# Mixture-of-experts stage: another order of the experts, two of them cut into 64 and 32 rows, and array tiles for the last two blocks and the products at the end

## The reference

```python
# hier_moe: t is (256, 1024); w_gate, w_up (32, 1024, 512); w_down (32, 512, 1024)
g_prob = softmax(t @ w_group + b_group); g_idx = argmax(g_prob)        # 4 groups
e_prob = softmax((t @ w_expert + b_expert)[group g_idx])               # 8 experts in the group
top_p, top_i = top_k(e_prob, 2)                                        # 2 experts for each token
top_w = g_gate * top_p / sum(top_p)
y = sum over the token's 2 experts e:  top_w * (silu(t @ w_gate[e]) * (t @ w_up[e])) @ w_down[e]
out = x + y
```

## Time and profile before

| | us |
|---|---|
| median of the runs | 1901.54 |
| the profiled execution itself | 1901.3 |
| its span, first to last instruction | 1899.5 |
| TensorE busy (matmul) | 1756.2 |
| VectorE busy | 1000.1 |
| ScalarE busy | 637.1 |
| first load of the experts' weights issued | at 1361.50 |
| first matmul of the first expert | at 1374.69 |
| granted TensorE clock, mean | 0.974 |

### The profile page before, as it was taken

The page is one execution under the profiler, slowest core; times in us unless marked ns, Lnnn a source line. Parts: engine busy times, 40 slices in busy tenths (PEclk is TensorE's granted clock), DMA queues, the critical chain, the costliest instruction groups (busy, mean ns, idle before and its releaser), DMA issues.

```text
span 1899.5 us, 22022 instructions
## 1 busy us (share of the span) xinstructions
PE 1756.2 (92%) x8277; PEld 1149.3 (61%) x8277; DVE 1000.1 (53%) x1751; ACT 637.1 (34%) x1140; POOL 93.3 (5%) x98
## 2 busy tenths in 40 slices
PE   7998999999999999999999998889699999966788
PEld 6887777777888877777774545554444443322232
DVE  5988555545678875555665896542522222111112
ACT  5543555454455445544534111220211111100001
POOL 1000000000000000000002121000000000000001
PEclk9999999999999999999999998989899999999899
DMA  7544434445555354443565343224388999999996
GB/s 244 167 145 132 145 112 134 115 123 162 149 178 176 111 166 122 120 137 100 169 182 162 110 155 100 83 73 129 128 334 373 368 395 420 420 420 421 420 421 246
DMA packets 131497, 392.60 MB, mean 207 GB/s; under 512 B 15567, under 2 KB 17379, under 8 KB 106817
## 3 DMA queue, kind: packets, MB, share of 16 engines
q1 hardware_dynamic: 126752, 386.64, 57.9%
q0 software_dynamic: 4640, 4.56, 0.8%
HBM read 387.73 MB, written 10.43 MB: 210 GB/s over the span
## 4 chain that ended last, share of the span: by engine, by line
PE 66%; DMA 13%; DVE 13%; ACT 4%; issue 3%; SPq 0%; POOL 0%; DVEq 0%; ACTq 0%; POOLq 0%
PE bank L749 11%; PE bank L698 10%; PE bank L700 10%; PE bank L699 10%; PE bank L1147 7%; PE bank L1164 5%; DMA r<-in_w_gate 3%; DVE w_lo L1251 3%; DMA spare<-in_w_gate 3%; DMA spare<-in_w_up 3%; DMA w_raw<-in_w_up 2%; DVE r L1251 2%; DVE r L1257 2%; PE bank L825 2%; PE bank L666 2%
## 5 line engine op out<-in xcount | busy, mean ns | idle before, releaser
L1251 DVE TENSOR_TENSOR w_lo<-w_raw,w_hi 128x1024 fp32r<-128x1024 f32 x266 | 320.7, 1217 | 225.4 <-ACT w_hi L2237 224.6
L698 PE MATMUL bank<-w_hi,h_hi 128*128 128x512 f32 x800 | 327.2, 409 | 14.4 <-DVE w_lo L1251 14.4
L2237 ACT CAST w_hi<-w_raw 128x1024 fp32r<-128x1024 f32 x266 | 277.5, 1048 | 164.3 <-PE bank L700 157.1
L700 PE MATMUL bank<-w_hi,h_lo 128*128 128x512 f32 x800 | 316.1, 395 | 0.0
L699 PE MATMUL bank<-w_lo,h_hi 128*128 128x512 f32 x800 | 315.5, 394 | 0.0
L698 PEld LDWEIGHTS bank<-w_hi,h_hi 128*128 128x128 f32 x800 | 152.6, 191 | 51.2 <-issue 15.2
L700 PEld LDWEIGHTS bank<-w_hi,h_lo 128*128 128x128 f32 x800 | 152.2, 190 | 33.7
L699 PEld LDWEIGHTS bank<-w_lo,h_hi 128*128 128x128 f32 x800 | 152.7, 191 | 29.1
L749 PE MATMUL bank<-w_raw,h_all 128*128 128x512 f32 (+1 forms) x320 | 142.4, 601 | 1.1 <-DVE h_all L1251 1.1
L2408 ACT ACTIVATE r<-bank,small 128x256 f32<-128x256 f32 (+1 forms) x152 | 63.8, 425 | 207.0 <-DVE small L1254 207.0
L2108 DVE TENSOR_REDUCE gate_t<-bank 128x128 f32<-128x512 f32 (+1 forms) x26 | 18.0, 692 | 189.4 <-PE bank L1129 189.4
(11 more groups left out here) (354 smaller groups left out, 2419.0 us busy)
## 6 DMA issues: line engine op xcount, KB each, us to landing
w_raw<-in_w_in SPq DMA_DIRECT2D x236, 512.0 KB, 3.7
w_raw<-in_w_proj SPq DMA_DIRECT2D x48, 512.0 KB, 3.7
r<-in_w_gate SPq DMA_DIRECT2D x20, 1024.0 KB, 22.2
r<-in_w_up SPq DMA_DIRECT2D x20, 1024.0 KB, 20.5
spare<-in_w_gate SPq DMA_DIRECT2D x19, 1024.0 KB, 23.2
spare<-in_w_up SPq DMA_DIRECT2D x18, 1024.0 KB, 20.8
spare<-in_w_down SPq DMA_DIRECT2D x14, 1024.0 KB, 23.8
w_raw<-in_w_down SPq DMA_DIRECT2D x14, 1024.0 KB, 25.9
```

Of the source, the lines that this page charges most:

```text
L698: e.matmul(out_, sh, mh, start=first, stop=False, skip_group_check=shared)
L700: return e.matmul(out_, sl, mh, start=False, stop=last, skip_group_check=shared)
L1251: o.did(v.tensor_tensor(out_, a, b, op), sem, value)
L2237: a.copy(halves(n)[0], raw_of(n)).then_inc(w_hi, 1)
```

## The change

- `RANKS` is another order. Before: 0, 15, 16, 1, 17, 18, 2, 19, 20, 3, 21, 4, 22, 5, 23, 6, 24, 7, 25, 8, 26, 9, 27, 10, 28, 11, 29, 12, 13, 14, 30, 31. After: four small ranks (15 to 18) behind rank 0, four (19 to 22) behind rank 1, three (23 to 25) behind rank 2, one behind each of ranks 3 to 6, and ranks 7 to 14 one after the other; 14, 30, 31 stay last.
- Ranks 5 and 6 become two blocks, of 64 and of 32 rows, in place of one of 128: 37 blocks.
- `FLAT` goes: `outer` of the last two blocks puts its two halves of the output side by side, in one bank, and ScalarE copies it in one instruction of 128 x 512.
- The products at the end take the output's first 512 columns from partitions 0 to 63 and the others from 64 to 127, so the two matmuls of a token tile stand in different rows of the array. The weights' matrix is made on all 128 partitions for that. The four adds and stores go by token tile first.
- Small tables move to make room for 37 columns in place of 35.

```diff
-RANKS = [0, 15, 16, 1, 17, 18, 2, 19, 20, 3, 21, 4, 22, 5, 23, 6, 24, 7, 25, 8, 26, 9, 27, 10, 28, 11, 29, 12, 13, 14, 30, 31]
-PARTS = {0: (0, P), 1: (0, P), 2: (0, P)}
+RANKS = [0, 15, 16, 17, 18, 1, 19, 20, 21, 22, 2, 23, 24, 25, 3, 26, 4, 27, 5, 28, 6, 29, 7, 8, 9, 10, 11, 12, 13, 14, 30, 31]
+PARTS = {0: (0, P), 1: (0, P), 2: (0, P), 5: (0, P // 2), 6: (0, P // 2)}
...
-    return P // 4 if most <= P // 4 and rank < EXP - 2 and FOUR else P // 2 if most <= P // 2 else P
+    return P // 4 if most <= P // 4 and rank < EXP - 2 else P // 2 if most <= P // 2 or PARTS.get(rank, (0,))[-1] == P // 2 else P
...
-                    n, ways = ROWS[x], 1 if FLAT[x] else WAYS[x]
+                    n, ways = ROWS[x], WAYS[x]
...
-                                done = e.transpose(bank[0:P // 2, c:c + P], last_by_token[:, w, t, :], ident)
+                                done = e.transpose(bank[:, c:c + P], last_by_token[:, w, t, :, :].rearrange("p d s -> p (d s)"), ident)
...
-                for n in range(2):
-                    await_drained(("down", last_blocks[0], n))
-                    for t in range(T):
+
+                def weighted(w, t, n, bank):
+                    part = slice(n * P // 2, (n + 1) * P // 2)
+                    return e.matmul(bank[:, :], last_weights[part, w, t, :], y_out[last_blocks[w] % 2][part, 0:CH], start=w == 0, stop=w == 1)
+
+                await_drained(("down", last_blocks[0], 0))
+                for t in range(T):
+                    for n in range(2):
                         _, bank = take(ends, ("end", t, n))
-                        e.matmul(bank[:, :], last_weights[:, 0, t, :], y_out[last_blocks[0] % 2][0:P // 2, n * CH:(n + 1) * CH], start=True, stop=False)
+                        weighted(0, t, n, bank)
                 outer(BLOCKS - 1, 0)
                 outer(BLOCKS - 1, 1)
...
+                await_drained(("down", last_blocks[1], 0))
+                for t in range(T):
+                    for n in range(2):
+                        weighted(1, t, n, banks[acc[("end", t, n)][0]]).then_inc(ends_summed, 1)
...
-                tt(of_last, of_last, last_by_token[:, 1, :, :], ADD)
-                o.prev()
-                tt(last_by_token, of_last.unsqueeze(1).to_broadcast([P, 2, T, P // 2]), last_mask.unsqueeze(2).to_broadcast([P, 2, T, P // 2]), MUL, last_in)
+                tt(of_last, of_last, of_second, ADD)
+                o.prev()
+                for i in range(2):
+                    tt(last_by_token[:, :, :, i, :], of_last.unsqueeze(1).to_broadcast([P, 2, T, P // 2]), last_mask.unsqueeze(2).to_broadcast([P, 2, T, P // 2]), MUL,
+                       last_in if i else None)
...
-                if WAYS[x] == 1 or FLAT[x]:
+                if WAYS[x] == 1:
```

More of the change, by code:

```diff
@@ L68 @@
 WAYS = [P // n for n in ROWS]
-FLAT = [r >= EXP - 2 for r in BLOCK_RANK]
 LOAD = [RANKS.index(r) for r in BLOCK_RANK]
@@ L574, in build @@
         last_blocks = (BLOCKS - 2, BLOCKS - 1)
[L575 to L578, removed]
+        last_by_token = scratch[1][:, :].rearrange("p (w t d s) -> p w t d s", w=2, t=T, d=2)
+        of_last, of_second = (scratch[3][:, i * P:(i + 1) * P].rearrange("p (t s) -> p t s", t=T) for i in range(2))
+        last_mask = scratch[3][:, 2 * P:3 * P].rearrange("p (w s) -> p w s", w=2)
+        last_weights = scratch[0][:, :].rearrange("p (w t s) -> p w t s", w=2, t=T)
         own_rows = [[R[i][:, 0:D], R[i][:, D:2 * D]] for i in (3, 6)]
@@ L589, in build @@
         block_rank, block_skip, block_last = (bias_rows[0][:, i * BLOCKS:(i + 1) * BLOCKS] for i in range(3))
-        count, offset = bias_rows[0][:, 108:140], bias_rows[0][:, 140:172]
+        count, offset = bias_rows[0][:, 116:148], bias_rows[0][:, 148:180]
         chosen_bf = nc.alloc_sbuf_tensor_at("chosen", [P, 2 * T * EXP], BF16, offset=starts["bias0"] + 4 * 240)
@@ L596, in build @@
         key = bias_rows[0][:, 432:464]
[L597 to L600, removed]
+        placed = bias_rows[1][:, 116:244].rearrange("p (c e) -> p c e", c=2)
+        position = bias_rows[1][:, 244:248]
+        start_f, before, beyond = (bias_rows[1][:, 248 + 38 * i:248 + 38 * i + BLOCKS] for i in range(3))
+        key_col, rank_col, count_col, offset_col = (bias_rows[1][0:EXP, 442 + i:443 + i] for i in range(4))
         expert_i = bias_rows[1][:, 464:464 + BLOCKS].bitcast(I32)
-        offset_all, count_all = (bias_rows[0][:, c:c + BLOCKS] for c in (304, 172))
+        offset_all, count_all = (bias_rows[0][:, c:c + BLOCKS] for c in (304, 180))
         order_cols = scratch[2][0:EXP, 0:EXP + 3 * BLOCKS]
         ahead, ahead_count = scratch[2][0:EXP, 160:192], scratch[2][0:EXP, 192:224]
-        position_i = bias_rows[1][:, 376:380].bitcast(I32)
-        start_i = bias_rows[1][:, 384:384 + BLOCKS].bitcast(I32)
-        row_i = bias_rows[1][:, 424:424 + BLOCKS].bitcast(I32)
+        position_i = bias_rows[1][:, 362:366].bitcast(I32)
+        start_i = bias_rows[1][:, 366:366 + BLOCKS].bitcast(I32)
+        row_i = bias_rows[1][:, 404:404 + BLOCKS].bitcast(I32)
         unit_row, lane, index_row = consts[:, 1088:1216], consts[:, 1267:1268], consts[:, 1218:1250]
@@ L2150, in moe @@
                         b, n, bank = await_full(("last",))
[L2151 removed]
+                        o.did(v.tensor_copy(last_weights.rearrange("p w t s -> p (w t s)"), bank[:, :]), drained[b], n)
                 for t in range(T):
@@ L2157, in moe @@
                 o.prev()
-                for n in range(2):
-                    for t in range(T):
-                        v.wait_ge(ends_summed, n * T + t + 1)
+                for t in range(T):
+                    for n in range(2):
+                        v.wait_ge(ends_summed, t * 2 + n + 1)
                         bank = banks[acc[("end", t, n)][0]]
@@ L2862, in sync_program @@
                         s.dma_start(PLACES[q % len(PLACES)], source[:, j * 2 * D:(j + 1) * 2 * D]).then_inc(in_moe[q % len(PLACES)], 16)
-            for n in range(2):
-                for t in range(T):
-                    s.wait_ge(x_final, n * T + t + 1)
+            for t in range(T):
+                for n in range(2):
+                    s.wait_ge(x_final, t * 2 + n + 1)
                     s.dma_start(out[t * P:(t + 1) * P, n * CH:(n + 1) * CH], x3[:, t, n * CH:(n + 1) * CH]).then_inc(stored, 16)
```

4 lines of the change are left out of this document (1 added, 3 removed).

## The result

| | before | after |
|---|---|---|
| median of the runs, us | 1901.12 (1899.32 to 1904.47, 4 runs) | 1886.32 (1884.05 to 1890.23, 4 runs) |
| the profiled execution, us | 1901.3 | 1886.12 |
| its span, us | 1899.5 | 1884.3 |
| mean granted clock | 0.974 | 0.972 |

The medians are 14.8 us apart, where 15.6 were forecast and 1885.9 was the predicted median. The ratio of the runs is 0.9917, with a 95% interval of 0.9897 to 0.9937, which is 15.8 us off, between 12.0 and 19.6.

What follows compares the result with a forecast made beforehand. The weight stream bounds the kernel: its start, its stops and the tail behind the last up piece set the end. Stream 6.7 plus tail 8.9 gives 15.6 us off 1901.3, 1885.7, or 1885.9 as a median; forecast's range 1882.7 to 1890.5.

Steps and rivals of the forecast that it cites:

- The bound: From 1580 us TensorE waits for the DMA; 421 GB/s, the most any window shows, is the stream's full rate.
- The first dip: Stream's stop at 1410 to 1424 us, waiting for rank 0's down piece: 9.6 us lost, unchanged by the new order.
- The second dip: Stream's stop at 1465 to 1481 us, waiting for rank 1's down piece: moves to about 1497, shrinks from 11.2 to 7.2 us.
- 2 to 3.5 us for a stretch: Length of TensorE's low clock (1.2 GHz) behind a wait, costing half its length; 1.7 us taken at rank 1.
- The third dip: Stream's stop at 1520 to 1538 us, 2.9 us lost: goes, with 3 us to spare at rank 2.
- The order's gain: Stream from the new expert order: 11.2 + 2.9 - 7.2 - 0.2 = 6.7 us earlier; bounds 2.1 to 9.3.
- The tail: Work behind the last up piece: 8.9 us shorter through faster outer and end products; bounds 6.8 to 9.5.
- The dip only moves: Rival: rank 1's new stop is as long as the two it replaces (14.1 us), only the end gains, 1892.6; chance 0.16.
- More goes: Rival: clock stays up behind rank 18, rank 1's stop under 4 us, small frictions go: 1880 to 1882; chance 0.10.
- Slower: Rival: rank 1 meets a cold TensorE whose clock stays at 1.2 GHz through both blocks, up to 1930; chance 0.03.
- The tiles that don't overlap: Rival at the kernel's end: end products' tiles don't overlap, 1888.0, or the last outer products' column tiles don't, 1892.8.

Runs made afterwards that it cites:

- The experiment with the five products: Kernel after, plus five unused 128x512 matmuls of constants in TensorE's idle time ahead of rank 1's first piece: 1883.0 us, ratio 0.9895 to the kernel before.

## Why the prediction was right, point by point

**The whole.** 14.8 us between the medians against 15.6 forecast. The profiled executions differ by 15.2, of which 1.0 is the untouched front; the two terms of the forecast's sum measure 5.2 and 9.0, 14.2 together. So the mechanism held, one term was 1.5 us too large, and that the predicted median (1885.9) is met within 0.4 us is in part luck.

**The bound.** The stream sets the time from 1377 us on, and what counts is where it stands still. The experiment with the five products holds to that: 2.5 us off a stop were 2.5 us off the stretch. The cut of ranks 5 and 6 took 6.5 us of work from TensorE and nothing from the time. One reading was too strict: 421 GB/s is not the most that any window shows (1366 to 1410 before has 422, windows of 2 us up to 430), but every stretch of 25 us and more without a stop lies at 420 to 422.

**The first dip** was to stay at 9.6 us and has 10.0 in a window of the same length. With its edges it is 9.9 before and 11.0 after, by the earlier issue told above and not by the order.

**The second dip** is the mis-sized term: 7.2 forecast, 8.7 measured. The forecast had the load issued 48.0 us behind rank 1's first matmul (46.0, 1.7 for the clock, 0.3 to the issue); it took from 1452.87 to 1502.25, 49.4. Of these 1.4 us, 0.8 are the clock: the first piece took 6.14 us for 3.60, so 2.5 in place of 1.7. The step that failed is "2 to 3.5 us for a stretch", worked out by spreading a mean of 0.95 over more than ten waits. Such a mean has short stretches in it beside long ones; the row behind a wait of about this length was a short stretch, as a window that follows the one shown there tells:

```profile
1668.00:1670.00 2.00, 2.00 (x16) 1.46 (x16) 1.00 (x2) 0.27 (x1) 0.00 (x0) 0.72 1.05 430
```

A mean of 0.72 is 1.1 us at the lower level, so there the clock came back some 3.1 us behind the first matmul. At rank 1 it stayed at 0.50 over all of 1451 to 1457, and the 2.5 us lost are 5.1 us of work at that level, an estimate from 6.14 and 3.60. This was no accident of one execution: in the six profiles with a wait of 4.75 to 5.17 us ahead of rank 1 the piece took 6.04 to 6.32. The experiment with the five products gave this loss back whole, 2.5 us. The other 0.6 are differences of about 0.1 us in each of the six terms between summed rows and the real row of two blocks.

The page "TensorE: Matmul & The Clock Gate" of the Trainium skill warned in its section "Why this matters for your kernels" against idle gaps between bursts of matmuls. The trace agrees: behind the gap of 4.89 us the clock was 0.50, and with the gap filled it was 1.00.

**The third dip** was to go and went: 420 GB/s from 1508 to 1580. Rank 2's first piece again met a low clock (5.15 us behind a wait of 4.76), and here it cost nothing, as the forecast had it with its 3 us to spare.

**The order's gain** by these steps: 6.7 forecast; measured 2.5 from the second dip (11.2 to 8.7) and 2.7 from the third (2.9 to 0.2), which is the 5.2 of the stretch, alone and in the whole change alike. The 0.2 that the forecast took off for more scatters is below what the rounded rates can show.

**The tail:** 8.9 forecast, 9.0 measured. Outer products 3.45 each, measured 3.60 and 3.65 with their drains; end products 1.9 each, measured 1.99. The gathered rows were there: the weighted adds began at 1872.97 behind the last three short operations, with no wait for them. The last four adds were counted at 0.74 each and took 0.60 from start to start, 2.48 together. The price was read wrongly: the pair of 1.48 in the earlier trace rows was not VectorE's own pace, its second add came when its product was done, and TensorE started its products 0.86 to 0.96 us apart. That made up for the small differences elsewhere.

**The rivals.** The dip only moves (14.1 us): fell, 8.7. More goes (a warm clock behind rank 18, a dip under 4 us): the clock fell as forecast. With the five products, which keep it up, the time was 1883.0, 1.0 us above the 1880 to 1882 that this rival gave, and the dip was 6.2. Slower, a clock that stays low through both blocks: the second row of rank 1 is at 10.46 for three pieces, full speed again. The tiles that don't overlap: fell on 1.99 us.

## What to carry to other kernels

When one engine's last use of a buffer releases a stream, every microsecond of the unbroken row of work ahead of that use counts in full (2.5 us of cold start there were 2.5 us of time), while 6.5 us of work taken off elsewhere were worth nothing: look for the load that was issued late and walk back from it. A TensorE gap of some 5 us before such a row can be worth filling with products that nobody reads; here five of them gave 2.5 us. A small order table, moved by a sum of pieces and their due times, gained 5 us, and putting half-filled products side by side in the array gained 9 where the chain of waits ran through them.

## What the runs showed of the hardware that was not expected

- Behind a wait of 4.89 us four matmuls of 128x512 took 6.14 us in place of 3.60, and behind one of 4.76 us 5.15: 2.5 and 1.5 us for nearly the same gap. Both repeat: 6.04 to 6.32 us at rank 1 in six profiles, 5.14 to 5.21 at rank 2 in four, while the run with the five products had 6.38 there (behind 4.77) and the one without the cut 6.69 (behind 3.11). The length of the gap alone doesn't give the price.
- Products that use different rows of the array overlap though they are not neighbours in the program. By the start records the third of four began 0.52 us ahead of the second. The page "TensorE: Matmul & The Clock Gate" of the Trainium skill, in its section "Packing small matmuls — row/col tiling", says that matmuls start and end in the order of the program. The start records of this case, in one profile, differ, and here the measurement decides; the ends are modelled in the profile and can't be used.
- VectorE's additions of 128x512 out of TensorE's banks followed each other at 0.60 us in a row of four, where a pair had taken 1.48 with its second add in step with TensorE's product.
- The front part of the program, the same in eight of these kernels, ended between 1368.6 and 1379.2 us in their profiles. Differences of 2 us between medians are less than that, and the two parts behind it together repeated within 0.2 us where the code is the same.
